# Two transformer blocks in one program: the modulation weights' ring from four places to eight, four tiles at a visit, and two pace tables

## The reference, cut to what matters

```python
def second_block(x, c, ctx, c_ctx, w_mod, b_mod, ...):
    s_lat, s_ctx, xc = silu(c), silu(c_ctx), ctx
    for i in range(DEPTH):
        mod, mod_c = s_lat @ w_mod[i] + b_mod[i], s_ctx @ w_mod[i] + b_mod[i]
        sh1, sc1, g1, sh2, sc2, g2 = split(mod, 6)
        h, hc = rms(x) * (1 + sc1) + sh1, rms(xc) * (1 + sc1c) + sh1c
        y, yc = token_mixers(h, hc, w_in[i], w_out[i], ...)
        x = x + g1 * y
        x = x + g2 * swiglu(rms(x) * (1 + sc2) + sh2, ...)
        # the context sequence the same in layer 0 alone
    return rms(x, final_norm)
```

## Time and profile before

| | us |
|---|---|
| median of 3 runs (1874.08 to 1878.76) | 1877.33 |
| the profiled execution: its own time | 1880.69 |
| its span from first to last instruction | 1879.4 |
| TensorE busy | 1807.4 (96%) |
| VectorE, ScalarE busy | 1276.7, 989.6 |

### The profile page before, as it was taken

How to read it: one execution, slowest core, us unless ns; L and a number is a source line. 1 busy time by engine, 2 the same in 40 slices (tenths; PEclk the granted TensorE clock), 3 DMA queues, 4 the chain that set the end, 5 groups by cost and what they waited for, 6 DMA issues and landing times. The chain is left out here.

```text
span 1879.4 us, 35697 instructions
## 1 busy us (share of the span) xinstructions
PE 1807.4 (96%) x14792; PEld 1669.2 (89%) x14792; DVE 1276.7 (68%) x2351; ACT 989.6 (53%) x1740; POOL 79.2 (4%) x78
## 2 busy tenths in 40 slices
PE   7999999999998999999999999999999999989997
PEld 6877799978898899999889897999999988779997
DVE  5556556568788755786766767766677777876665
ACT  4563544456555554564665655454455565644443
POOL 0000200010000200000110010000001000100000
PEclk9999999999999999999899999999999999989999
DMA  9778766887433465455454453455655543236663
GB/s 333 241 276 266 252 183 220 266 293 233 128 122 113 151 183 188 133 163 179 145 188 152 122 170 105 137 165 181 198 181 181 167 138 110 83 113 185 182 183 121
DMA packets 93825, 334.92 MB, mean 178 GB/s; under 512 B 10960, under 2 KB 12880, under 8 KB 93536
## 3 DMA queue, kind: packets, MB, share of 16 engines
q1 hardware_dynamic: 92016, 327.33, 54.7%
q0 software_dynamic: 1648, 5.31, 0.9%
HBM read 331.55 MB, written 1.05 MB: 177 GB/s over the span
## 5 line engine op out<-in xcount | busy, mean ns | idle before, releaser
L564 DVE TENSOR_TENSOR low<-ring,high 128x1024 fp32r<-128x1024 f32 x410 | 501.8, 1225 | 210.3 <-ACT high L556 199.7
L589 PE MATMUL bank<-XHx,high 128*128 128x256 f32 x2096 | 611.0, 291 | 23.1 <-DVE low L564 9.8
L590 PE MATMUL bank<-XLx,high 128*128 128x256 f32 x2096 | 595.1, 284 | 0.0
L591 PE MATMUL bank<-XHx,low 128*128 128x256 f32 x2096 | 594.9, 284 | 0.0
L556 ACT CAST high<-ring 128x1024 fp32r<-128x1024 f32 x410 | 428.2, 1045 | 290.7 <-PE bank L591 251.1
L589 PEld LDWEIGHTS bank<-XHx,high 128*128 128x128 f32 x2096 | 402.1, 192 | 44.9 <-issue 11.9
L590 PEld LDWEIGHTS bank<-XLx,high 128*128 128x128 f32 x2096 | 403.4, 192 | 1.1 <-issue 0.2
L591 PEld LDWEIGHTS bank<-XHx,low 128*128 128x128 f32 x2096 | 403.4, 192 | 0.0
L589 PE MATMUL bank<-XHc,high_side 128*128 128x256 f32 x608 | 181.6, 299 | 6.0 <-DVE low_side L564 4.4
L590 PE MATMUL bank<-XLc,high_side 128*128 128x256 f32 x608 | 172.5, 284 | 0.0
L591 PE MATMUL bank<-XHc,low_side 128*128 128x256 f32 x608 | 172.3, 283 | 0.0
(11 more groups left out here) (448 smaller groups left out, 3060.5 us busy)
## 6 DMA issues: line engine op xcount, KB each, us to landing
ring<-in_stream SPq DMA_DIRECT2D x410, 512.0 KB, 3.7
ring_side<-in_stream SPq DMA_DIRECT2D x110, 512.0 KB, 3.8
ring_mod<-in_stream SPq DMA_DIRECT2D x96, 512.0 KB, 5.7
x_nb<-in_rpb POOLq DMA_DIRECT2D x6, 256.0 KB, 3.4
x_late_NB<-in_rpb POOLq DMA_DIRECT2D x6, 256.0 KB, 3.2
Xx<-in_x SPq DMA_DIRECT2D x2, 512.0 KB, 5.9
Xc<-in_ctx SPq DMA_DIRECT2D x1, 1024.0 KB, 7.1
out<-y SPq DMA_DIRECT2D x8, 128.0 KB, 2.0
```

Source lines behind the costliest of these rows:

```text
L564: nc.vector.tensor_tensor(st.low[:, j % st.n_ring, :], st.ring[:, j % st.n_ring, :], st.high[:, j % st.n_split, :].bitcast(F32), ALU.subtr ...
L589: nc.tensor.matmul(out, wh, xh, start=(i == 0), stop=False)
L590: nc.tensor.matmul(out, wh, xl, start=False, stop=False)
L591: m = nc.tensor.matmul(out, wl, xh, start=False, stop=(c == ks[-1]))
```

## The change

The ring of modulation tiles has eight places, TensorE takes four tiles at a visit, and the table of due times asks for all 96 by 440 instead of 480. The eight places cover the memory of the side ring and side parts and, beyond it, of the contexts' high and low input parts `XHc` and `XLc`; for that, the context's buffers are laid out ahead of `x`'s. The contexts' table asks for 33 tiles by 830 (35 by 850 before) and all 110 by 1520 (1540 before).

```diff
-RING_MOD = 4
+RING_MOD = 8
@@ Program.__init__
-        for w in (x, c):
-            for n, name, dt in (("X", "NB", F32), ("XH", "T", F32R), ("XL", "PT", F32R)):
+        for w in (c, x):
+            for n, name, dt in (("XH", "T", F32R), ("XL", "PT", F32R), ("X", "NB", F32)):
@@
-MOD_US, MOD_BATCH = 0.43, 2
+MOD_US, MOD_BATCH = 0.43, 4
@@
-MOD_PLAN = [(0, 0), (480, MOD_TILES)]
-SIDE_PLAN = [(480, 0), (850, 35), (1300, 92), (1540, 110)]
+MOD_PLAN = [(0, 0), (440, MOD_TILES)]
+SIDE_PLAN = [(480, 0), (830, 33), (1300, 92), (1520, 110)]
```

## The result

| | before | after |
|---|---|---|
| median of the runs, us | 1877.86 | 1864.74 |
| the profiled execution: its own time | 1880.69 | 1861.59 |
| its span | 1879.4 | 1860.3 |
| TensorE busy | 1807.4 | 1791.5 |

The ratio is 0.9915 with a 95% interval of 0.9898 to 0.9932: about 16 us of 1878, faster by more than the 0.3% that can be told. One of the six runs of the changed kernel took 1974.65 us at a granted clock of 0.843; the ratio leaves it out, and the table's median counts it (1864.40 without). By the two medians the gain is 13 us, 0.9930, inside that interval. Run again later beside other kernels, the changed kernel stood at 1864.23 against 1879.40, ratio 0.9916 (0.9902 to 0.9930). The prediction was 1869.8 (1860 to 1883).

The account below looks back on a forecast made before the run. The prediction took TensorE as the bound, busy 1807.4 of 1879.4 us. Its terms summed to -7.5 us, taking the profiled 1880.69 to 1873.2; less 3.4 to the runs' median, that gave 1869.8 us, range 1860 to 1883.

Parts of the forecast that it names:

- Memory moves cost nothing: Buffer layout: no cost, since the side stream already waited for the last modulation and XHc, XLc are written later.
- Fewer places: TensorE's switches between weight products and modulations: fewer of them, at 0.19 us or half that each, save 2.8 us.
- Recurrence's stretch: Layer 0's recurrence: ends 2.3 us later but holds six tiles (3.0 us) more, so idle time changes by -0.7 us.
- the prediction's sentence on bandwidth: Recurrence loads: one core gets about 358 GB/s of HBM, so sixteen loads would take 1.8 us less than measured.
- First layer norm: Layer 0's first norm: both early visits ahead of the sums of squares, one after the last, saving 3.0 us.
- Second layer norm: Layer 0's second norm: idle time grows 2.0 us and a gap of some 4.5 us costs 3.0 us of clock.
- Behind it: Main work after layer 0's second norm, main tiles 100 to 110: no term of its own, 0 us.
- rival "slower": End of layer 0's second norm and contexts' new order: gaps without fillers lower the clock; +11.5 us, 1888.8, chance 0.14.
- Layer 1's second norm: Layer 1's second norm: 51 matmuls instead of 18 fill the gap, ending the wait and slow clock; -6.0 us.
- Elsewhere: Rest of the kernel: other waits on side tiles and a clock loss change by 0, with +-6 us.
- rival "a visit of four waits for four loads": Modulation visits: loads come no sooner, only places are saved, second norm's loss is paid; +2.2 us, 1879.5, chance 0.11.

Follow-up runs that it names:

- second and third set: Two later groups of follow-up kernels: one tested whether place in memory sets the time, the next tried other offsets of XHx and the ring alone undone.
- after_aligned: Changed kernel with both paths' small buffers moved behind the large ones, so XHx and XLx begin at a multiple of 1 KB again; 1873.62 us, ratio 0.9968.
- before_again: The kernel before, unchanged, run again as a yardstick; 1878.77 us, ratio 0.9994 against the kernel before.
- after_x512: Changed kernel with XHx and XLx beginning 512 bytes behind a multiple of 1 KB instead of 480; 1873.79 us, ratio 0.9967 against the kernel before.
- after_again: The changed kernel, unchanged, run and profiled once more; 1864.23 us, ratio 0.9916 against the kernel before.
- after_x960: Changed kernel with both paths' small buffers between the contexts' buffers and x's, so XHx and XLx begin at offset 960 instead of 480; 1846.14 us, ratio 0.9824.
- r8b4_oldside: Changed kernel with the contexts' table as before (35 by 850, 110 by 1540), modulations still due by 440; 1869.94 us, ratio 0.9946 against the kernel before.
- r8b4_oldplans: Changed kernel with both due-time tables as before, keeping eight places and four tiles at a visit; 1869.89 us, ratio 0.9934 against the kernel before.
- r4b4_newplans: Changed kernel with a ring of four places alone, keeping four tiles at a visit and both new tables; 1894.41 us, ratio 1.0086 against the kernel before.

## Why the prediction was right, and where it was wrong

The time fell inside the range and on the forecast's side. The sum had the right size for the order, and a term that it put at nothing was as large as the sum. By medians of the second and third set the edit splits like this: the order, at the old place in memory, 1873.6 - 1879.1 = **-5.5 us** (after_aligned, whose interval leaves -3.6 to -8.5; forecast -7.5); the place in memory, 1864.2 - 1873.6 = **-9.4 us** (forecast: "Memory moves cost nothing"). That sentence asked when buffers are written, and not where they then lie. The step that failed is this one. A hint stood in the profile after: 15.9 us less busy time for the same records. That the order's own sum came out near its forecast is in good part luck: by main tile 110 the terms that were priced add up to -1.5 in the forecast and measured +0.2, layer 1's norm gave 0.7 of its 6.0, and what is left was gained where the forecast had nothing (below).

For the order's terms the profiles at the same offset are compared: the mean of two executions of before (the first profile and before_again) with the mean of after_aligned and after_x512. The table gives the start of a main tile on TensorE, changed minus before, less 0.50 us for each modulation tile more and 24 x 0.1185 = 2.84 us for each context tile more that was done by then. In the kernel before, tile 24 starts near 126 us, 32 near 199, 110 near 455 and 128 near 585.

| main tile | 24 | 26 | 32 | 94 | 100 | 110 | 122 | 128 | 194 | 206 | 320 | 392 |
|---|---|---|---|---|---|---|---|---|---|---|---|---|
| us | +0.2 | -1.5 | -4.4 | -6.2 | -4.3 | +0.2 | +0.1 | -8.7 | -5.5 | -6.2 | -4.4 | -5.3 |

- **Fewer places** (forecast -2.8, from 0 to -3.8): up to tile 24 and from 32 to 94 it is +0.2 - 1.8 = -1.6, with the late loads that went. Right in sign; half price for all of them would have been closer.
- **Recurrence's stretch** (-0.7, from -3.0 to +1.0): -1.7 from tile 24 to 26. The last products start at 154.18, as forecast, but by another way. The sum let the sixteenth load go out 16 x 1.57 us after the first; 1.57 was the pace of a ring of four and not of the queue, and the visit that the sum let wait for that load starts at 151.32 without a wait. The 2 to 3 us for a landing were short as well: the tile's view of before has a median of 5.7. The Trainium skill, "HBM Reference", section Specifications (TRN2), says that one core streaming alone gets well above its share of 358 GB/s, some 425; the 403 GB/s from 130 to 140 us agree with that, and the 358 on which the prediction's sentence on bandwidth stood do not hold here.
- **First layer norm** (-3.0): -2.9 from tile 26 to 32. Right, and by its mechanism: both early visits stand ahead of the sums, one behind the last.
- **Second layer norm** (+5.0): +1.9 from tile 94 to 100. The gap came, and the lower clock behind it, but both smaller: 2.72 us of waiting instead of 4.5, and the products from 409.37 stand 0.21 us apart only until 412.8. From the last sum, at 403.7, the chain took 5.7 us, 6.3 in the forecast.
- **Behind it** (forecast 0): +4.5 from tile 100 to 110. Before, four modulation tiles filled a wait for `XLx` at the end of the gate, on TensorE's timeline before:

```profile
442.22 1.93 PE L723 MATMUL bank<-ring_mod,TMPc 128*32 128x256 f32 x32
```

  Now all tiles are spent by 402 and TensorE stands for 2.75 us at 436 to 439. It is the rival "slower" at another place: a filler that comes sooner is missing later. The rival named the end of the norm and priced it higher.
- **Layer 1's second norm** (-6.0): -0.7 from tile 194 to 206. This term failed. The 51 matmuls are there and run until 916.7, with 0.2 us of waiting on a side tile; but the gate's first product starts at 920.12 all the same. The last sum had come at 909.1, so the chain behind it took 11.0 us where it took 5.8 before. Releasers are inferred, and the row names `XLx`; an `XLx` was ready at 913.6, on VectorE's timeline after:

```profile
913.12 0.48 DVE L1229 SCALAR_TENSOR_TENSOR XLx<-Xx,par,XHx 128x256 fp32r<-128x256 f32 x1
```

  The `e` copy that empties the gate's bank ends at 920.02 on ScalarE's timeline, 0.10 us ahead of the product, as at the earlier trace rows, behind two rounding casts and two high parts:

```profile
916.45 1.03 ACT L557 CAST high_side<-ring_side 128x1024 fp32r<-128x1024 f32 x1
917.38 1.12 ACT L1207 ACTIVATE XHx<-Xx,par 128x256 fp32r<-128x256 f32 x2
918.41 1.03 ACT L557 CAST high<-ring 128x1024 fp32r<-128x1024 f32 x1
919.35 0.41 ACT L1362 ACTIVATE SQx<-e 128x256 f32<-128x256 f32 x1
919.67 0.35 ACT L1352 COPY e<-bank 128x256 f32<-128x256 f32 x1
```

  The step counted what fills the gap and took the chain as it was; the new order had lengthened the chain itself. That reading is from rows and was not tried, but four more profiles of this order (after_again, after_aligned, after_x512, after_x960) have it too: the copy ends 0.10 us ahead of the product and the first `XLx` 6.5 us ahead, where in the kernel before it is the first `XLx` that ends 0.05 us ahead and the copy 0.49. What improved is the clock: it stands at the lower level from 920.1 to 924.7, where it was 930.3 to 939.6 before.
- **Elsewhere** (0, with +-6): -8.8 from tile 122 to 128, given back in part (+3.2) by tile 194. The bound was too narrow, and the place was not the waits on side tiles that it was drawn from.

So of the order's -5.3 us, the modulations' own stretches gave 6.2 by tile 94 and lost 6.4 by 110; what is left at the end was won from 540 to 590 us, by no term of the sum, in a stretch that r8b4_oldside lost by a contexts' table with which r8b4_oldplans won it. Ring, visits and tables hold together: with four places the new tables cost 17 us, with eight places and four tiles at a visit they are worth 0.9916 / 0.9934, 3 us, within what the intervals leave open. The rival "a visit of four waits for four loads" did not decide: one wait of 0.4 us is left. With a ring of four it would have been worse than that rival had it: 1.0086 in r4b4_newplans against its +2.2 us.

## What to carry to other kernels

Where an edit moves a buffer that TensorE streams thousands of times, measure the move alone: here it was worth as much as the rest of the edit or more, and a small buffer put between two large ones gave another 1%. A queue's pace read from a trace belongs to its ring as long as loads wait for places; look for what each load waits for before calling it bandwidth. And fillers that are brought forward leave their old places empty: list those places, with the chain that each one covered.

## What the runs showed of the hardware that was not expected

- **The start of the streamed operand sets the products' distance.** In long runs without waits 119.98 ns at offsets 0 and 512 of `XHx`, 118.33 at 480, 113.37 or 117.77 at 960, all with the granted clock at 1.00. The Trainium skill, "TensorE: Matmul & The Clock Gate", section "Back-to-back issue gap", gives 262 cycles for 256 columns as the gap of isolated matmuls, which would be 109 ns at 2.4 GHz (an estimate from that page), and says that in a stream of weight loads and matmuls both set the distance. None of these long runs comes down to 109 ns, and they show a dependence on the offset that the section does not have.
- **DMA engines at 95% busy were not full.** The same engines moved 339 GB/s at a share of 0.95 and 403 at 1.01, with more loads under way; a load then took 7.2 us to land instead of 5.7 (medians of the tile's view), and TensorE waited for one load, 0.4 us.
- **After a wait of 2.75 us the clock fell with a delay.** From 439.03 the products ran at full distance for 1.4 us, and then from 440.4 to 443.4 at the lower level, 0.43 us apart instead of 0.23:

```profile
439.83 0.40 PE L629 MATMUL bank<-high,XHx 128*128 128x512 f32 x1
...
440.82 0.63 PE L629 MATMUL bank<-high,XHx 128*128 128x512 f32 x1
```
